# A mixture-of-experts step on one Trainium2 core: the first round's tokens are gathered already turned, and two sums move off VectorE's way to the selection

## The reference

```python
def moe(h, w_router, b_router, w_gate, b_gate, w_up, b_up, w_down, b_down):
    t = h.reshape(bsz * L, D)
    logits = t @ w_router + b_router
    top_v, top_i = lax.top_k(logits, TOP_K)          # 4 of 32 experts
    top_w = jax.nn.softmax(top_v, axis=-1)
    comb = jnp.sum(jax.nn.one_hot(top_i, N_EXPERTS) * top_w[..., None], axis=1)
    gate = jnp.einsum('td,edf->tef', t, w_gate) + b_gate
    up = jnp.einsum('td,edf->tef', t, w_up) + b_up
    gate = jnp.minimum(gate, SWIGLU_LIMIT)
    up = jnp.clip(up, -SWIGLU_LIMIT, SWIGLU_LIMIT)
    act = (up + 1.0) * gate * jax.nn.sigmoid(SWIGLU_ALPHA * gate) * comb[..., None]
    out = jnp.einsum('tef,efd->td', act, w_down) + comb @ b_down
    return out.reshape(bsz, L, D)

# in trunk_layer:
h2 = rms_norm(x, norm2_g) * (1.0 + scale2) + shift2   # what the experts read
x = x + gate2 * moe(h2, ...)
```

## Time and profile before

| what | value |
|---|---|
| median of 3 runs | 1088.86 us (1088.18 to 1089.82) |
| the profiled execution's own time | 1091.33 us |
| its span in the profile | 1089.5 us |
| TensorE busy | 934.8 us (86%) |
| VectorE busy | 403.4 us (37%) |
| ScalarE busy | 243.9 us (22%) |
| DMA | 445.45 MB, mean 409 GB/s |
| mean granted TensorE clock | 0.941 of full |

### The profile page before, as it was taken

How to read it: one execution, slowest core, us unless ns; L and a number is a source line. 1 busy time by engine, 2 the same in 40 slices (tenths; PEclk the granted TensorE clock), 3 DMA queues, 4 the chain that set the end, 5 groups by cost and what they waited for, 6 DMA issues and landing times.

```text
span 1089.5 us, 32878 instructions
## 1 busy us (share of the span) xinstructions
PE 934.8 (86%) x14006; PEld 564.0 (52%) x14007; DVE 403.4 (37%) x1016; ACT 243.9 (22%) x549; POOL 26.1 (2%) x34
## 2 busy tenths in 40 slices
PE   4999898999987969997878879999966999696975
PEld 2577665555553535653444455555533555353542
DVE  7999925333331313332222223333311333132323
ACT  5667524111110101110111111111100111011102
POOL 2002002000000000000000000000000000000000
PEclk9999998999998989998898999999978999898988
DMA  9759899999999999999999999999999999999995
GB/s 371 321 188 377 269 419 386 435 426 428 436 427 436 427 433 433 428 428 433 428 439 426 436 428 432 434 427 436 427 433 433 428 429 432 429 437 426 436 427 231
DMA packets 22083, 445.45 MB, mean 409 GB/s; under 512 B 2963, under 2 KB 3571, under 8 KB 5380
## 3 DMA queue, kind: packets, MB, share of 16 engines
q1 hardware_dynamic: 21348, 444.02, 96.2%
q10 hardware_dynamic: 384, 0.57, 0.1%
q0 software_dynamic: 320, 0.39, 0.1%
HBM read 443.09 MB, written 1.10 MB: 408 GB/s over the span
## 4 chain that ended last, share of the span: by engine, by line
PE 54%; DMA 35%; DVE 6%; issue 2%; ACT 1%; another core or an unknown queue 0%; SPq 0%; DVEq 0%; ACTq 0%
PE ps L1099 23%; DMA pair<-in_w_down 18%; PE ps L1133 14%; DMA pair<-in_w_up 11%; DMA pair<-in_w_gate 4%; DMA ring<-in_w_ada 3%; PE ps L1042 3%; PE ps L880 3%; PE ps L665 2%; PE ps L681 2%; PE ps L947 1%; DVE acts L1810 1%; DVE upc L1806 1%; DVE actT L1814 1%; DVE upc L1803 1%
## 5 line engine op out<-in xcount | busy, mean ns | idle before, releaser
L1099 PE MATMUL ps<-pair,XT 128*32 128x256 f32 x6528 | 402.6, 402 | 61.6 <-DMA pair<-in_w_gate 31.0
L1099 PEld LDWEIGHTS ps<-pair,XT 128*32 128x32 f32 x6528 | 222.6, 116 | 211.5 <-DMA pair<-in_w_up 34.5
L1133 PE MATMUL ps<-pair,actT 128*32 128x256 f32 x1600 | 103.5, 416 | 24.9 <-DMA pair<-in_w_down 24.0
L1471 ACT ACTIVATE sgm<-gcl 128x256 f32<-128x256 f32 x51 | 21.3, 417 | 426.7 <-DVE gcl L1801 426.7
L1803 DVE TENSOR_SCALAR upc<-ps 128x256 f32<-128x256 f32 x51 | 21.7, 425 | 229.8 <-PE ps L1099 229.8
L1133 PE MATMUL ps<-ring,actT 128*32 128x256 f32 x1664 | 95.8, 381 | 3.3 <-DMA ring<-in_w_down 1.7
L1475 ACT ACTIVATE selT<-ps 128x128 f32<-128x128 f32 x102 | 27.2, 273 | 313.6 <-PE ps L665 313.6
L1133 PEld LDWEIGHTS ps<-pair,actT 128*32 128x32 f32 x1600 | 57.3, 119 | 65.0 <-issue 36.6
L1827 DVE TENSOR_TENSOR ys<-ps,g2x 128x256 f32<-128x256 f32 x51 | 21.7, 425 | 144.0 <-PE ps L1133 144.0
L1133 PEld LDWEIGHTS ps<-ring,actT 128*32 128x32 f32 x1664 | 51.1, 110 | 41.6 <-DVE actT L1814 7.7
L1471 ACT ACT_TABLE_LOAD x50 | 64.2, 1283 | 3.8 <-issue 2.9
(11 more groups left out here) (293 smaller groups left out, 850.9 us busy)
## 6 DMA issues: line engine op xcount, KB each, us to landing
pair<-in_w_gate SPq DMA_DIRECT2D x32, 4096.0 KB, 29.7
pair<-in_w_up SPq DMA_DIRECT2D x32, 4096.0 KB, 35.2
pair<-in_w_down SPq DMA_DIRECT2D x16, 4096.0 KB, 38.6
ring<-in_w_down SPq DMA_DIRECT2D x31, 2048.0 KB, 39.0
ring<-in_w_ada SPq DMA_DIRECT2D x10, 2048.0 KB, 10.7
w<-in_w_in SPq DMA_DIRECT2D x2, 1536.0 KB, 19.6
wout<-in_w_out SPq DMA_DIRECT2D x1, 3072.0 KB, 12.5
wglu<-in_w_glu SPq DMA_DIRECT2D x1, 2304.0 KB, 11.2
```

Of the source, the lines that this page charges most:

```text
L1099: ins = pe.matmul(out[32 * fq:32 * fq + 32, :], XT[:, k % 2, (k // 2) * 32:(k // 2) * 32 + 32], tile_of(turn, m, k)[:, fq * QU:(fq + 1) * ...
L1133: ins = pe.matmul(pY[32 * dq:32 * dq + 32, :], actT[:, k % 2, (k // 2) * 32:(k // 2) * 32 + 32], tile_of(turn, 2, k)[:, dq * QU:(dq + 1) * ...
L1471: act.activation(sgm[:, :], gcl[:, :], ACT.Sigmoid, scale=1.702).then_inc(sem("sgm_ready"), 1)
```

## The change

Three things change, all at the start of the expert part.

1. The first round's tokens are gathered already turned. In place of `gather(0)`, ScalarE's copy and `turn_x(0)`, TensorE computes the turned tokens into `pT` directly: the stationary operand is a block of 128 columns of the tokens (every second column of a quarter of `h2`, or every eighth one of `h_mid` and `rb`), the moving one the 32 columns of `sel`.
2. For the second tile the products go over `h_mid` and `rb[:, 1]` apart, 8 products each, and are summed in PSUM. So there are 8 + 8 + 8 = 24 products. The first 8 go ahead of L1061's sum (`cu`), the other 16 behind it.
3. VectorE's two sums for the second half of `h2`, and `bias_row(0)`, go behind the selection. The wait for `h2_ready` 4 moves into the first round, ahead of `gather(R + 1)`. SyncE waits for `gathered` as well as `h2_ready` before it issues the last half of expert 1's w_down, since that load overwrites what the new products read.

```diff
@@ SyncE
             load_half(w_down[0, 1], 1, 0)
+            sp.wait_ge(sem("gathered"), 1)
             sp.wait_ge(sem("h2_ready"), 4)
             load_half(w_down[0, 1], 1, 1)
@@ TensorE
-            pe.wait_ge(sem("h2_ready"), 4)
-            gather(0)
+            def gather_turned(parts):
+
+                for x, tau, first_part, last_part in parts:
+                    for k in range(2):
+                        for kk in range(4):
+                            ins = pe.matmul(pT[:, k * P + 32 * kk:k * P + 32 * kk + 32], x(kk, k), sel[:, tau, :],
+                                            start=(first_part and k == 0 and kk == 0), stop=last_part, skip_group_check=True)
+                return ins
+
+            pe.wait_ge(sem("h2_ready"), 2)
+            pe.wait_ge(sem("hr_ready"), 4)
+            pe.wait_ge(sem("sel_ready"), 1)
+            gather_turned(((lambda kk, k: h2[:, 0, kk * QU + k:(kk + 1) * QU:2], 0, True, False),))
             pe.wait_ge(sem("rounds_ready"), 1)
             b = claim(pe, "cu")
             full(pe.matmul(b[0:NE, 0:1], C("triu", slice(0, NE))[:, 0:NE], cnt[:, 1:2], start=True, stop=True))
-            turn_x(0)
+            gather_turned(((lambda kk, k: h_mid[:, 2 * kk + k::8], 1, False, False),
+                           (lambda kk, k: rb[:, 1, 2 * kk + k::8], 1, False, True))).then_inc(sem("gathered"), 1)
@@ TensorE, expert_round
                         if bound is not None:
+                            pe.wait_ge(sem("h2_ready"), 4)
                             pe.wait_ge(sem("tables"), 1)
@@ ScalarE
-            empty_x(0)
-            act.wait_ge(sem("X_turned"), 1)
+            act.sem_inc(sem("Xs_ready"), 1)
+            act.sem_inc(sem("X_turned"), 1)
+            act.wait_ge(sem("gathered"), 1)
             act.copy(XT[:, :, :], pT.rearrange("p (n x) -> p n x", x=P)).then_inc(sem("XT_ready"), 1)
@@ VectorE
-            for b_ in range(2):
-                h = slice(b_ * HALF, (b_ + 1) * HALF)
-                dve.wait_ge(sem("hr_ready"), 3 + b_)
-                tt(by_k(1, b_), natural(h_mid[:, h]), natural(rb[:, 1, h]), ALU.add)
-                dve.sem_inc(sem("h2_ready"), 1)
...
-            bias_row(0)
@@ VectorE, behind rounds_ready
             dve.sem_inc(sem("rounds_ready"), 1)
+            for b_ in range(2):
+                h = slice(b_ * HALF, (b_ + 1) * HALF)
+                dve.wait_ge(sem("hr_ready"), 3 + b_)
+                tt(by_k(1, b_), natural(h_mid[:, h]), natural(rb[:, 1, h]), ALU.add)
+                dve.sem_inc(sem("h2_ready"), 1)
+            bias_row(0)
```

## The result

The changed kernel takes 1095.47 us (median of 6 runs, 1092.04 to 1097.18), the kernel before 1088.66 us (6 runs). The ratio is 1.0057, with a 95% interval of 1.0044 to 1.0071: 6.2 us slower, forecast 5.0.

A forecast was written before the change was run, and what follows sets the result against it. The prediction took the full weight queue (DMA, 430 GB/s from 178 us) as the bound. Late issues were to delay expert 2's w_gate by 3.8 to 5.5 us, taken as 5.0: 1088.86 + 5.0 = 1093.9 us, range 1088.5 to 1097.5.

The forecast's parts named there:

- the case of the empty queue: Expert 2's w_gate issued at about 202.3 into an empty queue: lands at 215.6, a loss of 5.5 us.
- The bound: Weight queue full from 178 us on at 430 GB/s; only a load issued too late, leaving it empty, costs time.
- Selection earlier: Ahead of the first round's gather: `sel` made sooner, TensorE starts at 184.95 in place of 186.26, 1.3 us earlier.
- The 24 products: First round's gather: each pass costs its weight load, 0.215 us; 16 passes take 3.45 us, the other 32 take 6.9.
- Which clock: TensorE during the new products: half clock (1.2 GHz) for all of them.
- The first gate products: Behind the gather: delayed 6.2 us, 5.54 us long as before, up to 0.3 more for the clock's edge.
- SyncE and w_gate: Last half issued at 195.7, expert 2's w_gate at about 202.3: w_gate lands 3.8 to 5.5 us later, taken as 5.0.
- Expert 3's w_gate: Issued at 231.3 behind a line that lands at 234.6: no second loss to speak of.
- The clock that rises during the products: Rival: the unbroken stream brings full clock at 188.8, passes of 0.123, loss 0.8 us, 1089.7 us; chance 0.16.
- The strided rival: Weight blocks of every eighth column load at half speed: 6.9 us more, loss 12.4, 1101.3 us; chance 0.10.
- The faster one: Rival: passes under 0.07 us end the gather sooner, 2.4 us gained in all, 1086.5 us; chance 0.03.

The follow-up runs named there:

- e3: The changed kernel with 12 products of 256 columns, `sel` as weights, then copy and turn, in place of the turned gather: 1089.49 us, 1.0008 to the kernel before.
- e7: The changed kernel with contiguous blocks of 128 columns of `h_mid` and `rb` as weights in place of every eighth column: 1092.34 us, 1.0041 to the kernel before.
- e9: The changed kernel with expert 1's w_up loaded in three pieces, as in e5: 1092.74 us, 1.0041 to the kernel before.
- e6: The kernel before with e5's three-piece w_up and e3's start (sums behind the selection, 12 wide products): 1086.29 us, 0.9976 to the kernel before.
- e1: The kernel before, with the last half of expert 1's w_down issued only when expert 0's gate products are done: 1091.09 us, ratio 1.0025.
- e4: The changed kernel with the selection repeated four times, so that 128 columns move in place of 32: 1093.96 us, 1.0046 to the kernel before.
- e2: The kernel before with the turned gather alone, 16 products of 32 columns over `h2`, last half issued on time: 1091.86 us, ratio 1.0027.
- e8: The changed kernel with both e4's 128 moving columns and e7's contiguous blocks: 1089.62 us, 1.0012 to the kernel before.
- e5: The kernel before with expert 1's w_up loaded in three pieces, the first two issued earlier: 1088.68 us, ratio 0.9999.

## Why the prediction was right

The forecast was a loss of 5.0 us and 1093.9 us; 6.2 and 1095.47 were measured. The mechanism was the one named, late issues into a queue that has run dry, and two things made the size short: the price of the strided passes (0.85 us), and 0.5 us that had been taken off the case of the empty queue.

**The bound.** That only the queue could carry a loss to the end held: in the table, the end follows w_gate's landing. The profile after shows the gaps at the two places named.

**Selection earlier.** Right to 0.01 us: the products start 1.40 us behind the ranking, 1.41 forecast. The moved sums ran under the products and cost nothing; e3 shows it for the times too.

**The 24 products.** The price came from L989's weight load, 0.215. Measured 0.22 for tile 0's 16 passes and 7.74 us for the 32 strided ones, 0.24 each, forecast 6.9. This term was 0.85 too small, and the first gate product starts 13.7 us behind the ranking, forecast 12.9.

**Which clock.** Right in this profile: 0.50 from about 177.3 to 197.8, and in the first window over the new products TensorE was busy without a break:

```profile
184.17:187.96 3.79, 3.79 (x18) 3.79 (x17) 1.23 (x6) 0.00 (x0) 0.00 (x0) 0.50 0.98 419
```

But the time at which it falls isn't fixed: in the profiles of e7 and e9 the first 16 passes still ran at full clock, and in e6's it never fell before the first gate products. The step took one profile's clock for all executions; that the profile after agreed so well is in part luck. The spread of the changed kernel, 5.1 us over 6 runs, fits with that. So does the kernel before beside e1 to e4: its 10 runs with a mean clock of 0.950 or more took 1087.4 us on average, the other 21 took 1088.8. No run here shows that the clock is the cause.

**The first gate products** took 6.1 us (192.78 to 198.86), forecast 5.54 and up to 0.3 more.

**SyncE and w_gate.** w_gate was issued 26.1 us behind w_up (18.9 before), 7.2 later, forecast 6.4. It landed 13.4 us behind its issue, the price of the empty queue. I had taken 5.0 between 3.8 and 5.5; the upper end was the right one (5.5 + 0.85 = 6.35, and 6.4 by the row). e1 shows what a late half costs alone, 2.7, and e2 what TensorE's delay costs alone, 2.9, with fewer products. The two don't add up in the changed kernel: in e2, with the half on time, w_gate landed 13.3 us behind its issue, and here 13.4, so by the profiles SyncE's wait for the gather adds next to nothing and the loss is TensorE's. No run takes that wait out of the changed kernel. Expert 3's w_gate lost nothing, as forecast: it was issued at 228.05, and the line ahead of it had until 212.5 + 19.5 = 232.0 to land.

**The rivals.** The clock that rises during the products was priced at 0.8 us with passes of 0.123; e4 made it rise, and 5.0 us of loss remained, since passes over strided blocks took 0.245 at full clock too. Its price was wrong for strided blocks, and in the changed kernel's profile its condition didn't hold. The strided rival has its mechanism (e4 against e8), but at half clock it is worth some 0.7 us (32 passes of 0.24 against 0.22), not the 6.9 priced. The faster one didn't hold: no narrow pass was under 0.12 us. The only version that gained closed the pause ahead of w_up as well (e6), which the prediction hadn't looked at.

## What to carry to other kernels

When one queue is full to the end, ask of each change only whether it moves an issue past the point where the queue runs dry; loads that nobody waits for count as well, if others stand behind them. A product whose moving side is narrow costs its weight load (0.22 us a pass here with 32 columns moving, at half clock), so turning the operands to save a transpose pays only where the weights stay few. Two steps that show no gain alone (e3, e5) can show one together (e6), so it is worth trying them together before they are dropped; how much of it is the clock stays open here.

## What the runs showed that I had not expected

Weight blocks with 32 bytes from column to column load no faster at 2.4 GHz than at 1.2: 0.245 us a pass against 0.24, where contiguous ones go from 0.22 to 0.12.

With the same unbroken stream of weight loads, the granted clock stayed at half for the whole gather with 32 columns moving (11.5 us in the changed kernel) and came back 5.5 us behind the first product with 128 columns (e4); in e8, whose first products still ran at full clock, 4.4 us behind it. The Trainium skill's "TensorE: Matmul & The Clock Gate", What's actually happening, speaks of how busy TensorE has been; TensorE shows as fully busy in all three, so the busy time of the profile doesn't tell them apart. These are single profiles, and which property of the products matters was not tried further. The changed kernel over its gather, then e4 ahead of the rise and behind it:

```profile
180.46:191.92 11.46, 11.46 (x50) 11.32 (x50) 3.42 (x13) 1.75 (x4) 0.00 (x0) 0.50 0.77 328
```

```profile
181.16:186.56 5.40, 5.40 (x24) 5.16 (x25) 3.17 (x12) 1.28 (x4) 0.00 (x0) 0.50 0.96 410
186.80:192.80 6.00, 6.00 (x27) 5.96 (x25) 0.04 (x1) 0.00 (x0) 0.00 (x0) 1.00 0.43 182
```

The part of the program ahead of the experts, equal in all kernels, ends up to 4.3 us sooner or later from one execution to the next (w_up issued from 172.7 to 177.0), which is two thirds of what this change costs. Why was not tried.
